# Prompt attention of a hybrid decoder step: TensorE takes the values of the unit three back ahead of the transposes of the unit two back

## What is computed

```
s_s = q . k_selected * HEAD_DIM ** -0.5        p_s = masked_softmax(s_s)        o_s = p_s @ v_selected
s_w = q . k_window   * HEAD_DIM ** -0.5        p_w = masked_softmax(s_w)        o_w = p_w @ v_window
out = gate[0] * o_c + gate[1] * o_s + gate[2] * o_w      # o_c: compressed branch, done earlier
```

## Time and profile before

| | |
|---|---|
| median of three runs | 1475.15 us |
| the profiled execution's own time | 1467.87 us |
| its span | 1466.2 us |
| TensorE busy over the span | 98% |
| ScalarE / VectorE busy over the span | 28% / 57% |
| first scores of the stage to the end of its last values | 671.5 to 781.8 us |
| granted TensorE clock in the stage | 1.00 |

### The profile page before, as it was taken

How to read it: one execution, slowest core, us unless ns; L and a number is a source line. 1 busy time by engine, 2 the same in 40 slices (tenths; PEclk the granted TensorE clock), 3 DMA queues, 4 the chain that set the end, 5 groups by cost and what they waited for, 6 DMA issues and landing times.

```text
span 1466.2 us, 30386 instructions
## 1 busy us (share of the span) xinstructions
PE 1438.5 (98%) x12380; PEld 1138.4 (78%) x12380; DVE 837.8 (57%) x1634; ACT 409.4 (28%) x888; POOL 184.5 (13%) x256
## 2 busy tenths in 40 slices
PE   9999999999999999999999999999999999999997
PEld 8887578878888866886668668888788888888886
DVE  7665058633433446315774537677666766666664
ACT  3112372123233215216775631102211011101001
POOL 1000324532222212205001310000000000000000
PEclk9999999999999999999999999999999999999999
DMA  6222543211111247447001974422222222222221
GB/s 264 87 87 72 181 167 114 93 61 46 47 47 42 95 160 233 148 132 237 32 2 53 325 297 147 140 94 87 73 86 86 75 84 87 85 73 97 90 86 61
DMA packets 57399, 163.94 MB, mean 112 GB/s; under 512 B 7312, under 2 KB 19696, under 8 KB 55952
## 3 DMA queue, kind: packets, MB, share of 16 engines
q1 hardware_dynamic: 48608, 121.46, 25.2%
q0 software_dynamic: 7936, 39.40, 7.6%
q10 hardware_dynamic: 720, 1.16, 0.2%
HBM read 144.01 MB, written 22.15 MB: 113 GB/s over the span
## 4 chain that ended last, share of the span: by engine, by line
PE 93%; DVE 3%; ACT 1%; issue 1%; DMA 0%; SPq 0%; DVEq 0%; ACTq 0%
PE acc L1049 26%; PE acc L1194 14%; PE acc L1980 5%; PE acc L2008 5%; PE acc L1989 5%; PE acc L1219 5%; PE acc L2033 4%; PE acc L1142 2%; PE acc L1335 2%; PE acc L1157 2%; PE acc L1735 2%; PE acc L1747 2%; PE acc L1631 1%; PE acc L1758 1%; PE acc L1352 1%; PE acc L1061 1%
## 5 line engine op out<-in xcount | busy, mean ns | idle before, releaser
L1049 PE MATMUL acc<-sb_work,sb_ring 128*128 128x272 f32 x602 | 150.8, 392 | 0.0
L2530 ACT ACTIVATE sb_omemT<-acc 128x272 f32<-128x272 f32 x74 | 29.3, 396 | 386.1 <-PE acc L1980 234.5
L1049 PE MATMUL acc<-sb_work 128*128 128x272 f32 x530 | 133.0, 393 | 0.0
L1049 PEld LDWEIGHTS acc<-sb_work,sb_ring 128*128 128x128 f32 x602 | 114.4, 190 | 23.6
L1049 PEld LDWEIGHTS acc<-sb_work 128*128 128x128 f32 x530 | 100.5, 190 | 21.4 <-issue 0.8
L1194 PE MATMUL acc<-sb_work,sb_ring 128*128 128x272 f32 x360 | 93.3, 399 | 2.9 <-DVE sb_work L2739 2.9
L1194 PEld LDWEIGHTS acc<-sb_work,sb_ring 128*128 128x128 f32 x360 | 66.4, 190 | 17.9 <-issue 4.4
L1980 PE MATMUL acc<-sb_work,sb_ring 128*128 128x272 f32 x308 | 77.2, 393 | 1.0 <-issue 1.0
L1219 PE MATMUL acc<-sb_work,sb_ring 128*128 128x272 f32 x320 | 77.7, 395 | 0.0
L1989 PE MATMUL acc<-sb_work,sb_ring 128*128 128x272 f32 x308 | 77.1, 392 | 0.0
L1219 PEld LDWEIGHTS acc<-sb_work,sb_ring 128*128 128x128 f32 x320 | 59.7, 190 | 14.9 <-issue 3.3
(11 more groups left out here) (491 smaller groups left out, 2771.9 us busy)
## 6 DMA issues: line engine op xcount, KB each, us to landing
sb_ring<-w_stream SPq DMA_DIRECT2D x144, 512.0 KB, 3.5
sb_work<-pages SPq DMA_DIRECT2D x56, 192.0 KB, 4.2
branch_gates<-sb_work SPq DMA_DIRECT2D x24, 272.0 KB, 2.7
sb_work<-branch_gates POOLq DMA_DIRECT2D x8, 816.0 KB, 14.9
sb_ring<-w_stream SPq DMA_DIRECT2D x16, 384.0 KB, 3.4
sb_work<-mem_kT SPq DMA_DIRECT2D x8, 512.0 KB, 8.4
sb_work<-mem_v SPq DMA_DIRECT2D x8, 512.0 KB, 10.6
query_features<-sb_work SPq DMA_DIRECT2D x10, 272.0 KB, 3.6
```

What stands on the lines that cost most here:

```text
L1049: mm = pe.matmul(out, w[:, q, :], x[q], start=q == 0, stop=q == n - 1)
```

## The change

The three parts of a turn of TensorE's loop change their order. Before, a turn is scores u, transposes u-2, values u-3. After, it is scores u, values u-3, transposes u-2. In the turns 36 and 37 memory scores, transposes, values become memory scores, values, transposes. The waits stay where they belong: the one for `sb_done` is ahead of the first transposes still, the one for `sw_done` ahead of the first values. Instructions, buffers and the other engines' orders are the same.

```diff
             for u in range(2, N_ATT + 3):
                 if u < N_ATT:
                     att_scores(u)
+                if N_ATT <= u < N_ATT + 2:
+                    memory_scores(u - N_ATT)
                 if u == 2:
                     pe.wait_ge(sb_done, 1)
-                if u < N_ATT:
-                    att_turn(u - 2)
                 if u == 3:
                     pe.wait_ge(sw_done, 1)
-                if N_ATT <= u < N_ATT + 2:
-                    memory_scores(u - N_ATT)
-                    att_turn(u - 2)
                 if u >= 3:
                     att_values(u - 3)
+                if u < N_ATT + 2:
+                    att_turn(u - 2)
```

## The result

The changed kernel takes **1473.99 us** (median of 20 runs, 1471.41 to 1482.02), the kernel before 1469.34 us (20 runs, 1466.84 to 1475.57). The two medians differ by 4.65 us. The ratio estimated from all runs is 1.0028 with an interval of 1.0016 to 1.0040: 4.1 us, with 2.4 to 5.9 inside the interval. So slower is established. On which side of the forecast's bound of 0.3% the change lies isn't settled: the ratio says 0.28%, the medians 0.32%, and the interval holds both.

The account below looks back on a forecast made before the run. The prediction took the stage as bound by TensorE's own work, with four weight-shape changes a unit instead of three. Terms of +3.15, +1.2, -2.9, +1.55, +1.0 and +1.1 gave +5.1 us: 1480.3 us, +0.35%, range 1475.0 to 1485.0.

Parts of the forecast that it names:

- Term 1: TensorE's mask, now followed by values of another weight shape: +0.09 us a turn, 35 turns, +3.15 us.
- Term 2: Transposes now follow another weight shape and load their first weights in the open: 0.05 us, 24 times, +1.2 us.
- Term 3: Transposes' waits for scaled probabilities go, hidden by the values now ahead: -2.9 us.
- Term 4: Values wait for ScalarE's copy, 0.20 at j5 and 0.11 at j3, five times each: +1.55 us.
- Term 5: Scores of j3 wait for j1's exponentials, which ScalarE runs after j5's copy: +0.20 five times, +1.0 us.
- Term 6: Last unit's values follow their own transposes at once: a wait of 1.26 where 0.17 stood, +1.1 us.
- The hidden change of shape: Rival, chance 0.14: weight loads run ahead at mask to values and values to transposes; sum +0.75, 1475.9 us.
- Only the old waits go: Rival, chance 0.03: copies are in time and no drain is paid; -2.9, 1472.3 us.
- The copy becomes the loop: Rival, chance 0.20: copy, exponentials, scaling and transposes of j1 close a ring; +3.6 more, 1483.9 us.
- Transposes wait as long as before: Rival, chance 0.05: their exponentials come later by a copy, so the old waits stay; +8.0, 1483.2 us.

Follow-up runs that it names:

- e3: Kernel before with the mask's products ahead of the scores' products, no values moved: stage 128.38 us against 126.41 before.
- e5: Changed kernel without the two semaphore increments ahead of the scores and the values: stage 130.29 us, 1.07 shorter.
- e1: Changed kernel with values ahead only in the turns of j1 and j4, whose transposes waited, old order elsewhere: stage 125.35 us against 126.4 before.
- e4: Changed kernel with the last unit's values moved behind the third memory scores: stage 130.06 us, 1.30 shorter.
- e6: Changed kernel with ScalarE taking the exponentials of a unit ahead of the copy: stage 144.37 us, 13.0 longer.
- e8: Kernel before without the two semaphore increments ahead of scores and values: stage 126.33 us against 126.41.
- e7: e1 with the late last values of e4 and without the increments, as in e5: stage 125.17 us, median 1472.05 us, ratio to before 1.0027.
- e10: e7 with the increments put back, each behind the first product of its group: stage 125.22 us, median 1466.99 us, ratio to before 1.0011.

## Why the prediction was right, and where it was wrong

**The mechanism held, term by term.**
- What bounds the kernel: TensorE's own order. Right; a head pair's +0.84 is found whole in the distances of TensorE.
- Term 1, +0.09 a turn for mask to values: measured 0.09 with 256 columns (0.32 against 0.23) and 0.10 with 128 (0.22 against 0.12). e3 shows the cost of the fourth change with the values left in place, and e5 that it isn't the increment. The tenth is shown; that the engine drains there no trace shows by itself.
- Term 2, 0.05 for the open first load: measured 1.02 against 0.97 for eight transposes. Right.
- Term 3, the old waits: 3.5 became 1.0. The six left have at most 0.2 each; the forecast said none but the start's. They move no start: such a load waits 0.17 at 722.79, but the values ahead of these transposes take their usual 0.59 (722.20 to 722.79). e1 gives the other side: where only these waits are treated, the stage is 1.06 shorter.
- Term 4, waits for the copy: 0.21 at j5 (forecast 0.20) and 0.10 at j3 (0.11). No other unit waits. Right.
- Term 5, the scores of j3 behind the exponentials of j1: 0.21 (forecast 0.20). Right.
- Term 6, the last values: a wait of 1.21 (forecast 1.26, so +1.1), and e4 takes 1.30 out. Right.
- Behind the stage nothing takes the delay in. Right.

The sum was +5.1, the stage measured +4.95, and a head pair +0.84 instead of +0.79. The interval of the runs' +4.1 holds 4.95; whether the rest gives some of it back, these runs can't say, since the difference is smaller than what executions vary by.

**The step that failed is the base.** The prediction put +5.1 on the median of three runs, 1475.15, with the words that the profiled execution's 7.3 less is "within what executions differ by". The sum had been made against that execution, and twenty runs of before have their median at 1469.34, close to its 1467.87 and 5.8 below the base that was taken. That alone puts 1480.3 where 1473.99 was measured, and even the range's lower end, 1475.0, lies above the result. On the median of twenty the same sum gives 1474.4, on the profiled execution 1473.0. That the last is only 1.0 off is partly luck: its base is 1.5 too low, and its 5.1 is 0.45 more than the medians differ by. Two of the first three runs, 1475.15 and 1475.57, are among the three longest of the twenty. A hole like that of 560 to 580 us, worth some 7 us, would explain such runs, but no long run of before was profiled, so that stays open.

The other doubtful step is the side of the bound. "Slower by over 0.3%" had 0.55 and "same" 0.43, with a sum only 0.7 above the bound of 4.4. The runs put the change at 4.1 by their ratio and 4.65 by their medians, so they don't settle the side. The sum was 1.0 or 0.45 too large, inside what these runs can tell.

**The rivals.** The hidden change of shape is out by e3, and by the distances. "Only the old waits go" is out with it. "The copy becomes the loop" did not happen (a head pair grew by 0.84, and not by 1.4), but e6 shows that it is near: the exponentials of one unit ahead of the copy make it 13 us. "Transposes wait as long as before" is out by the waits view.

## What to carry to other kernels

Moving one group of products ahead of another on a full TensorE is two sums: the waits that it hides, and the changes of weight shape that it adds, each about a tenth of a microsecond here, every turn. Here 35 turns paid for 11 waits of 0.2 to 0.6, so the swap belongs only in the turns that wait (e1). Put such a sum on the execution whose rows it was made from, or on a median of many runs, not on one of three.

## What the runs showed of the hardware that was not expected

- **A semaphore increment on TensorE behind a wait costs about 0.09 us when the wait is a real one** (e5: 0.66 to 0.57, 0.30 to 0.21, 1.21 to 1.11), and nothing measurable without a wait (e8: a head pair takes 17.28 as before).
- **In three kernels with 72 instructions fewer a later stretch was slower.** Without the increments TensorE has one wait on "issue" of 3.51, 3.78 and 4.06 us (e5, e7, e8) some 54 us behind the stage, where before, after and e10 have 1.2 to 1.9. Behind it the granted clock is lower for the next products. At that point the DMA engines are full in before as well: the windows of before and after for it are

```profile
840.80:846.20 5.40, 4.39 (x134) 3.22 (x127) 5.16 (x7) 1.90 (x4) 0.00 (x0) 1.00 1.03 398
```

```profile
853.00:859.00 6.00, 4.83 (x150) 3.48 (x143) 5.72 (x11) 2.33 (x4) 0.00 (x0) 1.00 1.03 398
```

with a DMA share of 1.03. What the waits are for can be read from the profile's DMA queues, in windows of half a microsecond. One queue is called "q8 instruction" and carries packets of 0.02 MB. Its line in the window 849.0 to 849.5 of e7 (packets, MB, share of 16 engines):

```profile
q8 instruction: 1, 0.02, 12.9%
```

In e7 one starts at 849.0 to 849.5 and TensorE goes on at 851.45; in before they start at 843.5 to 844.0 and 849.0 to 849.5, and TensorE goes on at 846.39 and 851.92; in e8 at 848.5 to 849.0, and at 851.17. In all twelve traces each of TensorE's waits on "issue" between 797 and 875 us ends 2.2 to 2.6 us behind the start of such a packet. I read them as waits for TensorE's instructions. Other such packets are followed by no wait, where TensorE still has work. That the packets come late because the queues are full, and that 72 instructions fewer move the place where TensorE runs out of them, is argued and not shown: e10 speaks for it, but no run moved the number in steps, or put other instructions in the increments' place.
- **A stretch of 20 us ahead of the stage (560 to 580) falls to a granted clock of 0.83 in some executions of kernels with and without the change**, and the stage then starts about 7 us later (678.75 and 678.86 in after and e3; 671.3 to 673.0 in the other ten). It begins with a store that ScalarE waits for, `branch_gates<-sb_work`, which takes 17.2 and 17.7 us to land, where it took 13.8 in before. What makes the store late was not tried.
